# Latent attention of a two-block model on one core: heads computed in pairs, positional products in the two row halves

## The reference, cut to what matters

```python
for blk in range(s // ATTN_BLOCK):
    lo, hi = blk * ATTN_BLOCK, (blk + 1) * ATTN_BLOCK
    sc = (jnp.einsum('bqhd,bkhd->bhqk', q_nope[:, lo:hi], k_nope[:, :hi])
          + jnp.einsum('bqhd,bkd->bhqk', q_rope[:, lo:hi], k_rope[:, :hi])) * scale
    sc = jnp.where(kpos[None, :] <= qpos[:, None], sc, -jnp.inf)
    p = jax.nn.softmax(sc, axis=-1).astype(v.dtype)
    outs.append(jnp.einsum('bhqk,bkhd->bqhd', p, v[:, :hi]))
...
return (o.reshape(b, s, MLA_V) * jax.nn.silu(gate)) @ w_out
```

## Time and profile before

| | |
|---|---|
| time, median of 3 (lowest to highest) | 1984.59 us (1983.8 to 1985.16) |
| time of the profiled execution | 1984.39 us |
| its span in the trace | 1982.6 us |
| mean granted TensorE clock | 0.961 |
| PE busy | 1868.6 us (94%), 8760 instructions |
| PEld / DVE / ACT / POOL busy | 1520.0 / 898.7 / 744.6 / 870.2 us |
| the stage of the change | about 1810 to 1917 us of the span |

### The profile page before, as it was taken

One profiled execution on the slowest core, in us unless ns is written; L12 is line 12 of the kernel. 1 busy time (PEld: TensorE's weight loads), 2 busy tenths in 40 slices (PEclk: granted clock), 3 DMA queues, 4 the chain that ended last, 5 costly groups with the idle time before them and its releaser, 6 DMA issues.

```text
span 1982.6 us, 24835 instructions
## 1 busy us (share of the span) xinstructions
PE 1868.6 (94%) x8760; PEld 1520.0 (77%) x8760; DVE 898.7 (45%) x1301; ACT 744.6 (38%) x1168; POOL 870.2 (44%) x1159
## 2 busy tenths in 40 slices
PE   2869999999999999999999999999999999799995
PEld 1857888888888766788888888778888878577784
DVE  7996232121225789342121225642255541556644
ACT  7223343232324467433232324413233242334651
POOL 1023555555545621355555545554454445262231
PEclk8559999999999999999999999999999999899997
DMA  3243323333333321133333332322222223131111
GB/s 142 48 112 114 107 92 96 106 88 104 96 96 88 112 64 33 64 96 96 100 91 98 104 93 88 103 80 84 95 76 84 75 84 105 49 106 54 43 43 42
DMA packets 49439, 171.03 MB, mean 86 GB/s; under 512 B 5952, under 2 KB 6336, under 8 KB 48704
## 3 DMA queue, kind: packets, MB, share of 16 engines
q1 hardware_dynamic: 47936, 167.06, 27.7%
q10 hardware_dynamic: 1424, 2.88, 0.5%
HBM read 161.27 MB, written 2.10 MB: 82 GB/s over the span
## 4 chain that ended last, share of the span: by engine, by line
issue 44%; POOL 37%; PE 11%; DVE 3%; ACT 2%; DMA 1%; POOLq 1%; SPq 0%; ACTq 0%
POOL wlo L426 37%; PE ps L827 2%; PE ps L829 2%; PE ps L828 2%; PE ps L1222 1%; PE ps L1213 1%; PE ps L1212 1%; ACT u L502 1%; PE ps L875 1%; DMA yg<-vsb 1%; DMA d<-in_d 1%; PE ps L993 1%; PE ps L867 0%; PE ps L854 0%; DVE bt L321 0%
## 5 line engine op out<-in xcount | busy, mean ns | idle before, releaser
L426 POOL TENSOR_TENSOR wlo<-raw,whi 128x256 fp32r<-128x256 f32 x1152 | 859.3, 778 | 1069.0 <-ACT whi L457 1069.0
L457 ACT ACTIVATE whi<-raw 128x1024 fp32r<-128x1024 f32 x288 | 301.9, 1052 | 376.2 <-PE ps L829 374.1
L827 PE MATMUL ps<-Ch,whi 128*128 128x512 f32 x912 | 363.3, 398 | 0.5 <-POOL wlo L426 0.5
L829 PE MATMUL ps<-Ch,wlo 128*128 128x512 f32 x912 | 356.0, 390 | 0.0
L828 PE MATMUL ps<-Cl,whi 128*128 128x512 f32 x912 | 355.6, 390 | 0.0
L827 PE MATMUL ps<-Ah,whi 128*128 128x512 f32 x656 | 265.1, 404 | 9.7 <-DVE Al L1427 8.0
L829 PE MATMUL ps<-Ah,wlo 128*128 128x512 f32 x656 | 256.9, 392 | 0.0
L828 PE MATMUL ps<-Al,whi 128*128 128x512 f32 x656 | 256.7, 391 | 0.0
L827 PE MATMUL ps<-Bh,whi 128*128 128x512 f32 x640 | 250.6, 392 | 0.0
L829 PE MATMUL ps<-Bh,wlo 128*128 128x512 f32 x640 | 249.4, 390 | 0.0
L828 PE MATMUL ps<-Bl,whi 128*128 128x512 f32 x640 | 249.3, 390 | 0.0
(11 more groups left out here) (336 smaller groups left out, 2096.6 us busy)
## 6 DMA issues: line engine op xcount, KB each, us to landing
raw<-in_w SPq DMA_DIRECT2D x288, 512.0 KB, 3.6
u<-in_xch SPq DMA_DIRECT2D x1, 2048.0 KB, 10.1
yg<-vsb SPq DMA_DIRECT2D x16, 128.0 KB, 2.3
yg<-zz SPq DMA_DIRECT2D x16, 128.0 KB, 2.3
h<-in_xfm SPq DMA_DIRECT2D x2, 1024.0 KB, 5.7
out<-h SPq DMA_DIRECT2D x8, 256.0 KB, 2.0
bB<-in_bc SPq DMA_DIRECT2D x1, 1024.0 KB, 5.6
bC<-in_bc SPq DMA_DIRECT2D x1, 1024.0 KB, 11.9
```

Source lines behind the costliest of these rows:

```text
L426: last = nc.gpsimd.tensor_tensor(wlo[:, r, cc], raw[:, r, cc], whi[:, r, cc].bitcast(F32), ALU.subtract)
L457: nc.scalar.activation(whi[:, slot, :], raw[:, slot, :], ACT.Copy).then_inc(hi_ready, 1)
L827: nc.tensor.matmul(out, whi[:, slot, w], xh, start=first, stop=False)
L829: return nc.tensor.matmul(out, wlo[:, slot, w], xh, start=False, stop=last)
```

## The change

Units are renumbered in pairs of heads: the two heads of a pair take turns within a block (`unit3`: head `2*(un//8) + un%2`, block `un//2 % 4`). `scores3` now takes a pair of units: it waits until both banks of scores are free, runs the two `qn`-`kn` matmuls over 128 rows, then the two positional matmuls, one in rows 0 to 63 and one in rows 64 to 127, and posts both units by one increment of 2 behind the last. TensorE calls it once every two turns, for the pair after the present one. The zero padding of the rotated key and the two memsets go, and the sum that writes it is one instruction; a pad keeps all addresses. The values rotate over three banks. A head's gated output goes to `sg` or `std` by turns, and `gated`, `low` and `high` of the two heads of a pair come at turns 0, 1 and 2 of the next pair of heads; those of the last two heads follow the loop.

```diff
+        def unit3(un):
+            return 2 * (un // (2 * NB)) + un % 2, un // 2 % NB
+
+        def gout(hh):
+            return (sg, std)[hh % 2][:, :]
+
+        OB = (SX, SY, SZ)
...
-            def scores3(un):
-                hh, n = un // NB, un % NB
-                pe.wait_ge(rope_done, 19 + hh // 2 + 1)
-                if un >= 2:
-                    pe.wait_ge(sc_out, PAIRS + un - 1)
+            def scores3(pair):
+                jp, n = pair // NB, pair % NB
+                pe.wait_ge(rope_done, 19 + jp + 1)
+                if pair:
+                    pe.wait_ge(sc_out, PAIRS + 2 * pair)
                 keys, qs = (n + 1) * P, slice(n * P, (n + 1) * P)
-                nc.tensor.matmul(ps[:, un % 2, 0:keys], qn[:, hh, qs], kn[:, hh, 0:keys], start=True, stop=False)
-                nc.tensor.matmul(ps[:, un % 2, 0:keys], qr[:, hh // 2, qs], krz[:, hh % 2, 0:keys], start=False, stop=True).then_inc(sc_ps, 1)
+                for b in range(2):
+                    nc.tensor.matmul(ps[:, b, 0:keys], qn[:, 2 * jp + b, qs], kn[:, 2 * jp + b, 0:keys], start=True, stop=False)
+                for b in range(2):
+                    r = slice(64 * b, 64 * b + 64)
+                    last = nc.tensor.matmul(ps[:, b, 0:keys], qr[r, jp, qs], kr[r, 0:keys], start=False, stop=True)
+                last.then_inc(sc_ps, 2)
...
-            for un in range(3):
-                scores3(un)
+            scores3(0)
             pe.wait_ge(vt_done, 18)
             for un in range(U3):
                 strip_part("mgate", un // 4, un % 4, "A")
-                if un + 3 < U3:
-                    scores3(un + 3)
+                if un % 2 == 0 and un + 2 < U3:
+                    scores3(un // 2 + 1)
                 pe.wait_ge(p_ready, U1 + un + 1)
...
-                    for b in range(2):
-                        r, z = slice(64 * b, 64 * b + 64), slice(64 - 64 * b, 128 - 64 * b)
-                        V.memset(krz[z, b, :], 0.0)
-                        last = V.tensor_tensor(krz[r, b, :], ev[r, 0, :], ev[r, 1, :], ALU.add)
-                    last.then_inc(rope_done, 1)
+                    V.tensor_tensor(kr[:, :], ev[:, 0, :], ev[:, 1, :], ALU.add).then_inc(rope_done, 1)
...
                 normed3(un)
-                if un % NB == 1 and un > NB:
-                    gated(un // NB - 1)
-                if un % NB == 2 and un > NB:
-                    low("C", un // NB - 1, sg[:, :])
+                if un >= 2 * NB:
+                    if un % (2 * NB) in (1, 2):
+                        low("C", un // (2 * NB) * 2 - 3 + un % (2 * NB), gout(un - 1))
+                    if un % (2 * NB) < 2:
+                        gated(un // (2 * NB) * 2 - 2 + un % (2 * NB))
...
-            gated(MH - 1)
-            dve.wait_ge(o_out, MH)
-            low("C", MH - 1, sg[:, :])
+            for hh in (MH - 2, MH - 1):
+                gated(hh)
+                dve.wait_ge(o_out, hh + 1)
+                low("C", hh, gout(hh))
```

More of the change, by code:

```diff
@@ L227, in program @@
             qr = area(st, "qr", [P, 4, TOK])
-            krz = area(st, "krz", [P, 2, TOK])
-            kr = krz[:, 0, :]
+            krz = area(st, "kr", [P, TOK])
+            kr = krz[:, :]
+            area(st, "pad_k", [P, TOK])
             v3 = area(st, "v3", [P, NB, D])
@@ L787, in exp3 @@
             def exp3(un):
-                n, q0 = (un % NB + 1) * P, 8 * (un % SLOTS)
+                n, q0 = (unit3(un)[1] + 1) * P, 8 * (un % SLOTS)
                 asked()
@@ L799, in _ @@
             for un in range(U3):
-                n = (un % NB + 1) * P
+                n = (unit3(un)[1] + 1) * P
                 if un + 2 < U3:
@@ L806, in _ @@
                     gates(un // NB - 1)
-                if un % NB == 1 and un > NB:
-                    act.wait_ge(o_out, un // NB)
-                    high("C", un // NB - 1, sg[:, :])
+                if un % (2 * NB) < 2 and un >= 2 * NB:
+                    hh = unit3(un)[0] - 2
+                    act.wait_ge(o_out, hh + 1)
+                    high("C", hh, gout(hh))
                 if un % NB == 2:
@@ L812, in _ @@
             gates(MH - 1)
-            act.wait_ge(o_out, MH)
-            high("C", MH - 1, sg[:, :])
+            for hh in (MH - 2, MH - 1):
+                act.wait_ge(o_out, hh + 1)
+                high("C", hh, gout(hh))
             post("oout")
@@ L1204, in _ @@
             pe.wait_ge(evac, OUT0["mgate"])
-            def scores3(un):
-                hh, n = un // NB, un % NB
-                pe.wait_ge(rope_done, 19 + hh // 2 + 1)
-                if un >= 2:
-                    pe.wait_ge(sc_out, PAIRS + un - 1)
-                keys, qs = (n + 1) * P, slice(n * P, (n + 1) * P)
-                nc.tensor.matmul(ps[:, un % 2, 0:keys], qn[:, hh, qs], kn[:, hh, 0:keys], start=True, stop=False)
-                nc.tensor.matmul(ps[:, un % 2, 0:keys], qr[:, hh // 2, qs], krz[:, hh % 2, 0:keys], start=False, stop=True).then_inc(sc_ps, 1)
+            def scores3(pair):
[3 more added lines that the diff above has]
+                    pe.wait_ge(sc_out, PAIRS + 2 * pair)
+                keys, qs = (n + 1) * P, slice(n * P, (n + 1) * P)
+                for b in range(2):
[4 more added lines that the diff above has]
+                last.then_inc(sc_ps, 2)
             def values3(un):
-                hh, n = un // NB, un % NB
+                hh, n = unit3(un)
                 pe.wait_ge(pt_ready, U1 + un + 1)
-                if n == 0 and hh >= 2:
-                    pe.wait_ge(o_out, hh - 1)
+                if n == 0 and hh >= len(OB):
+                    pe.wait_ge(o_out, hh - len(OB) + 1)
                 for kb in range(n + 1):
-                    last = nc.tensor.matmul(ps[:, SX + hh % 2, n * P:(n + 1) * P], v3[:, kb, hh * P:(hh + 1) * P], ev[:, un % 2, kb * P:(kb + 1) * P],
+                    last = nc.tensor.matmul(ps[:, OB[hh % 3], n * P:(n + 1) * P], v3[:, kb, hh * P:(hh + 1) * P], ev[:, un % 2, kb * P:(kb + 1) * P],
                                             start=(kb == 0), stop=(kb == n))
@@ L1236, in _ @@
                     pe.wait_ge(pt_ready, U1 + un - 1)
-                transposes(sm3[:, un % SLOTS, :], 2 + un % 2, un % NB + 1).then_inc(pt_ps, 1)
+                transposes(sm3[:, un % SLOTS, :], 2 + un % 2, unit3(un)[1] + 1).then_inc(pt_ps, 1)
                 if un:
@@ L1841, in gated @@
                 dve.wait_ge(silu_done, 8 + hh + 1)
-                V.tensor_tensor(sg[:, :], ps[:, SX + hh % 2, :], sg3[:, hh, :], ALU.mult).then_inc(o_out, 1)
+                dve.wait_ge(x_lo, xs[0])
+                V.tensor_tensor(gout(hh), ps[:, OB[hh % 3], :], sg3[:, hh, :], ALU.mult).then_inc(o_out, 1)
             masked_max3(0)
```

## The result

The changed kernel takes 2017.76 us (median of 4 runs, 2016.45 to 2018.09) against 1984.21 us before: a ratio of 1.0165, 95% interval 1.015 to 1.0179. It is slower, by 33 us. The forecast was 2011.4 us, +27.0, with a range to 2019.

A forecast was written before the change was run, and what follows sets the result against it. It took TensorE's instruction queue, full in the last layer's attention, as the bound. From 1984.39 us, -8.7 (halves) + 3.6 (visits) + 30.4 (even-turn waits) + 1.7 (odd turns) = +27.0 gave 2011.4 us, range 2003 to 2019.

The forecast's parts named there:

- Part 2: Even turns of the last layer's attention: TensorE waits for DVE's chain behind the paired scores, 15 waits, 30.4 us.
- part 1: Positional products: two heads side by side in row halves save 8.7 us, less 3.6 us charged for 16 visits.
- The rival of free visits: Going in and out of the row halves costs nothing, so the 3.6 us go: 2007.8 us; chance 0.05.
- Part 4: Memsets and sum taken from DVE, three value banks, and gating of the last two heads behind the loop: taken as nothing.
- dearer visits, bare weight loads and the tail: Upper unknowns of the range: visits fully exposed +3.0, 0.1 us of weight load behind 18 waits +1.8, loop's end +1.
- halves don't run side by side: Positional products in row halves would not overlap at all: 2016.5 us, inside the range; no chance of its own given.
- a clock below 1.00 in the stage: Listed sign that the forecast is wrong: TensorE's granted clock under full level during the last layer's attention.
- the clock falls: In the stage, because TensorE stands about 1.9 us in every 8: 2015 to 2040 us; chance 0.06.
- the comparison with one row: Ahead of a fall near 799 us TensorE was busy 2.76 of 5 us; here near 6.2 of 8, hence chance 0.06.
- Part 3: Odd turns: DVE's chain is covered, except behind block 1 of the later three pairs of heads, 0.56 us each, 1.7 in all.
- faster than before: Waits don't arise if DVE's norm came ahead of the mask, or scores a turn earlier: 1979.3 us; chance 0.04.

The follow-up runs named there:

- padded: The changed kernel, but with positional products over all 128 rows with the zero-padded key as before; 2023.29 us, ratio 1.0181.
- early_norm: The changed kernel with scores of a pair a turn earlier and, on DVE in even turns, the norm ahead of the mask; 1981.24 us, ratio 0.9978.
- early_norm_padded: The changed kernel with scores a turn earlier, DVE's norm ahead of the mask in even turns, and the zero-padded key over 128 rows; 1985.65 us, ratio 1.0001.
- unit_by_unit: The changed kernel's numbering, three banks and later gating, but scores unit by unit three ahead and the padded key; 1983.85 us, ratio 0.9993.
- the pair without waits: early_norm and early_norm_padded: the changed kernel with earlier scores and norm, with row halves and with the padded key; 1981.24 and 1985.65 us.
- filled: The changed kernel with six unused 128x512 products more behind the scores in each even turn; 2014.79 us, ratio 1.0144.
- filled_later: The changed kernel with six unused products in even turns and ScalarE's split of the weight strip a turn later; 2014.0 us (two runs).
- norm_first: The changed kernel with only DVE's queue turned round: in even turns the norm ahead of the mask of the unit two ahead; 2001.08 us, ratio 1.0074.

## Why the prediction was right, and where it was short

**Right: the direction, the mechanism, the place.** Part 2, the lost lead, is the cause, shown from both sides: taken from the kernel before it makes 79.7 us, given back to the changed kernel it takes back all. With the odd turns it put 32.1 us of waits, counted from the end of the products' stream; the list of waits, which counts from their modelled end, has 30.1: 28.2 in the 15 even turns and 1.9 in three odd ones. The four chains, worked out for sizes that the kernel before never had side by side, came within 0.01 us.

**Right: part 1.** Halves run side by side, and each visit costs part of the gain. Behind a wait the 16 visits cost 3.5 us, where 3.6 was charged, and the halves are worth 5.2 us, not 5.1 (padded). Bare, in and out cost 0.34 us instead of 0.41, so the halves would be worth 3.3 us there, not 2.1 (early_norm). The rival of free visits would have made early_norm_padded 8.7 us slower than early_norm in the stage; it is 3.3. The Trainium skill, in TensorEngine Tiling (Array Packing), section Theoretical Speedup, gives up to 2x for a contraction of 64 or less; here 3.3 of the 8.7 us come back without a wait behind the visits, 5.2 with one.

Part 4 at nothing is what unit_by_unit shows for the banks and the end of the loop. That the memsets were worth nothing is not tested alone; the stage begins at 1811.06 us without them and at 1810.12 with them, so nothing of the 2 us came back.

**Short by 6.3 us** (33.3 in the stage, 27.0 forecast). The time lies inside the range, and that is in part luck. The range was built from dearer visits, bare weight loads and the tail, up to +5.8; what filled it was something else. By the time alone the rival "halves don't run side by side", 2016.5, fits even better than the forecast; it is padded and the pair without waits that rule it out. And a clock below 1.00 in the stage stood on the prediction's own list of signs of being wrong. Three terms were missing or too small:
- The clock, which the prediction held for a rival of 0.06, "the clock falls". It did, but in a smaller measure than the earlier trace rows let expect: 3.4 us at a time and 1.3 us each, 4.0 in all (filled). The step that failed is the comparison with one row: PE was busy 55% there, and 66 to 78% in the stretches ahead of the falls here. A share that is higher than the one row does not exclude a fall. The row was short, too: in the kernel before PE was busy 12.17 of the 19 us from 780 to the fall at 799, 64%, close to what stands ahead of the falls here.
- Part 3, the odd turns. The durations were taken from rows in which POOL does not work beside the norm. The new order lays POOL's strip beside it: 1.6 us (filled_later).
- The remaining 0.8 us (0.7, and the 0.1 by which part 1 came out better) are not traced to a cause; 18 waits, each with a slower first transpose behind it (0.16 instead of 0.11 us for one), would give 0.9.

**Wrong: the conditions that the rival "faster than before" named.** DVE's order alone (norm_first) is not enough, as said above; the scores a turn earlier are, for a tie, and both together for a gain.

## What to carry to other kernels

When a producer's work is issued in larger groups, look at what the group's end does to the consumer's queue. Here DVE (the consumer of the scores) had the mask of a unit of the new group ahead of the norm that TensorE (their producer) waits for, and a lead of a turn was lost without any wait being added to the code. Count waits per turn from rows of dependent chains, even for sizes that never stood side by side. And where a full TensorE begins to wait, put the clock in the sum, not among the rivals.

## What the hardware showed that was not expected

- The clock fell to the lower level with PE busy 66 to 78% in the stretches ahead and no wait longer than 2.3 us, and it held for 76 us at 78% behind them; in filled, with 128.40 of 135.80 us, it did not fall. Six unused products in each wait shortened the stage by 4.0 us.
- A DVE scaling from SBUF to SBUF of 128x256 elements takes 0.35 us alone and took 0.87 us in three places while GpSimd works; the scaling from PSUM right behind it (L1461), with GpSimd still at work, takes its usual 0.68. Moving GpSimd's work by a turn gave the 0.35 back in all eight. Not every such scaling beside GpSimd is long: in early_norm the one of 128x128 elements at 1862.69 us takes 0.30, with GpSimd at work from 1861.48 for 2.82 us.
- Going into the 64-row halves and out again costs 0.34 us in sum, more than the halves save for 128 keys (0.23 us), and 0.22 us where a wait stands behind the way out.
